# Three weight panels abreast behind each inner norm, and a fourth from tiles of its own, in a hybrid decoder layer

## The reference

```python
def layer_norm(x, g, b):
    xf = x.astype(jnp.float32)
    mu = jnp.mean(xf, axis=-1, keepdims=True)
    xc = xf - mu
    var = jnp.mean(xc * xc, axis=-1, keepdims=True)
    return xc * lax.rsqrt(var + LN_EPS) * g + b
...
    m = jnp.concatenate([y_pool, y_sgu], axis=-1) @ w_out
    h = layer_norm(ALPHA * h + m, ln1_g, ln1_b)
    h = layer_norm(ALPHA * h + mem_attend(h, mem_k, mem_v, w_mq, w_mo), ln2_g, ln2_b)
    h = layer_norm(ALPHA * h + peer_ffn(h, peer_wq, peer_subkeys, peer_u, peer_v), ln3_g, ln3_b)
```

## Time and profile before

| | us |
|---|---|
| median of 3 runs (3997.79 to 4003.11) | 3999.24 |
| the profiled execution | 3993.57 |
| its span, first to last instruction | 3991.8 |
| TensorE busy (matmuls) | 3829.6, 96% |
| VectorE busy | 2589.6, 65% |
| ScalarE busy | 1322.9, 33% |
| GpSimd busy | 784.2, 20% |
| load of an output projection panel, issue to landing | 6.1 |

### The profile page before, as it was taken

One profiled execution on the slowest core, in us unless ns is written; L12 is line 12 of the kernel. 1 busy time (PEld: TensorE's weight loads), 2 busy tenths in 40 slices (PEclk: granted clock), 3 DMA queues, 4 the chain that ended last, 5 costly groups with the idle time before them and its releaser, 6 DMA issues.

```text
span 3991.8 us, 61700 instructions
## 1 busy us (share of the span) xinstructions
PE 3829.6 (96%) x24133; PEld 3710.8 (93%) x24133; DVE 2589.6 (65%) x3361; ACT 1322.9 (33%) x1615; POOL 784.2 (20%) x509
## 2 busy tenths in 40 slices
PE   8998999979979979999999999999999999999997
PEld 6798999979857979999999999999999999999997
DVE  3423343351463356678888577777898998889896
ACT  3342222131342133232455422222233333333334
POOL 0000020020000030027300012222433233433440
PEclk9999999989989999999999999999999999999999
DMA  6542332223543212234455799999999999999994
...
DMA packets 392241, 941.40 MB, mean 236 GB/s; under 512 B 24356, under 2 KB 264672, under 8 KB 339992
## 3 DMA queue, kind: packets, MB, share of 16 engines
...
HBM read 865.84 MB, written 72.77 MB: 235 GB/s over the span
## 4 chain that ended last, share of the span: by engine, by line
PE 88%; DVE 5%; DMA 4%; ACT 2%; DVEq 1%; issue 1%; POOL 0%; SPq 0%; ACTq 0%
PE pp L197 25%; PE pp L1163 23%; PE pp L1210 13%; PE pt L1210 7%; PE pl L1210 7%; PE pt L1137 2%; PE pp L816 2%; DMA u_raw<-in_peer_ut 1%; PE pt L816 1%; PE pl L816 1%; DVE gbuf L1989 1%; PE pp L883 1%; DMA kv<-in_cache_mem_k 1%; DMA raw<-in_w_mk 1%; PE pl L845 1%
## 5 line engine op out<-in xcount | busy, mean ns | idle before, releaser
L1163 PE MATMUL pp<-h_hi,ut_hi 128*128 128x384 f32 x2048 | 703.5, 343 | 1.4 <-DVE ut_lo L1887 1.4
L1163 PE MATMUL pp<-h_lo,ut_hi 128*128 128x384 f32 x2048 | 690.2, 337 | 0.0
L1163 PE MATMUL pp<-h_hi,ut_lo 128*128 128x384 f32 x2048 | 688.5, 336 | 0.0
L212 DVE TENSOR_TENSOR w_lo<-raw,w_hi 128x2048 fp32r<-128x2048 f32 x120 | 274.8, 2291 | 470.1 <-ACT w_hi L207 470.1
L1535 ACT ACTIVATE v_hi<-v_raw 128x1024 fp32r<-128x1024 f32 x256 | 271.8, 1062 | 671.6 <-PE pp L1210 491.3
L1887 DVE TENSOR_TENSOR ut_lo<-u_raw,ut_hi 128x1024 fp32r<-128x1024 f32 x256 | 331.8, 1298 | 248.5 <-ACT ut_hi L1503 168.9
L1163 PEld LDWEIGHTS pp<-h_hi,ut_hi 128*128 128x128 f32 x2048 | 385.4, 188 | 2.1 <-DVE ut_lo L1887 1.7
L2012 DVE TENSOR_TENSOR v_lo<-v_raw,v_hi 128x1024 fp32r<-128x1024 f32 x256 | 314.1, 1227 | 110.5 <-ACT v_hi L1535 109.4
L1163 PEld LDWEIGHTS pp<-h_lo,ut_hi 128*128 128x128 f32 x2048 | 385.4, 188 | 0.0
L1163 PEld LDWEIGHTS pp<-h_hi,ut_lo 128*128 128x128 f32 x2048 | 384.7, 188 | 0.0
L207 ACT ACTIVATE w_hi<-raw 128x2048 fp32r<-128x2048 f32 x120 | 229.3, 1911 | 411.2 <-PE pp L197 285.5
...
## 6 DMA issues: line engine op xcount, KB each, us to landing
...
```

What stands on the lines that cost most here:

```text
L212: nc.vector.tensor_tensor(w_lo[:, s], raw[:, s], w_hi[:, s].bitcast(F32), ALU.subtract).then_inc(lo_ready, 1)
L1163: last = mm(pp[0][:, d, 0:N], w[:, d, k, :], x[:, k, S:S + N], start=(k == 0 and w is ut_hi and x is h_hi), stop=(k == KC - 1 and w is ut_lo))
```

## The change

**GpSimd's subtraction goes.** VectorE subtracts the mean itself in `dve_apply`, directly before each `yt`, with a drain between the two. `pool_less_mean` and its semaphore go.

**Splits.** ScalarE splits the second panel behind the norm ahead of the last square and not behind it. Panels three and four get tiles of their own: `wx_hi[0]`, `wx_lo[0]` and `wx_hi[1]`, `wx_lo[1]`, in the space of `y_hi`/`y_lo` that is free by then. ScalarE and VectorE fill the first between the mean copy and the reciprocal, the second in the middle of the norm's loop (after chunk 9 on ScalarE, after chunk 11 on VectorE).

**TensorE.** `behind_norm` multiplies three panels chunk by chunk, the third into `pl`. `fourth_panel` follows, from the `wx` tiles into the two banks of `pt`. The loop of panels goes on from the fifth. In the expert query stage the scorings of the first five panels are written out: the first stands in the middle of the fourth panel, the third in the middle of the fifth; the third panel's queries have a tile of their own, `q2x`.

**Waits.** The cache loads wait for three query panels in place of the projection's end. GpSimd clears its part of `sc` in two pieces, the second after three scorings.

Its core (the rest changes counts of semaphores and the number of panels skipped):

```diff
+        def pe_panel(pe, u, x_hi, x_lo, first=False, n=T, middle=None):
...
+                if middle is not None and k == KC // 2:
+                    middle()
...
+        def act_split_ahead(act, u):
+
+            s = u % 2
+            act.wait_ge(raw_in[s], num(u)[2])
+            act.wait_ge(panel_done, u - 2 - s)
+            nc.scalar.activation(wx_hi[s][:, :, :], raw[:, s], ACT.Copy).then_inc(hi_ready, 1)
+
+        def dve_split_ahead(dve, u):
+
+            s = u % 2
+            dve.wait_ge(hi_ready, u + 1)
+            nc.vector.tensor_tensor(wx_lo[s][:, :, :], raw[:, s], wx_hi[s][:, :, :].bitcast(F32),
+                                    ALU.subtract).then_inc(lo_ready, 1)
...
+                    if less:
+                        nc.vector.tensor_tensor(buf[:, c, :], buf[:, c, :], flat(mu[:, :, :]), ALU.subtract)
+                        dve.drain()
                     nc.vector.tensor_tensor(yt[:, c % 2, :], buf[:, c, :], flat(rs[:, :, :]), ALU.mult)\
                         .then_inc(nsem["yt"], 1)
...
             pairs(act, u0, KC, body, skip_first=4)
+            act_split(act, num(u0 + KC + 1))
             act_square(act, nm, KC - 1, 1)
-            act_split(act, num(u0 + KC + 1))
             act_mean(act, nm)
+            act_split_ahead(act, u0 + KC + 2)
...
-        def pool_less_mean(pool, nm, buf=r):
-            nm.wait(pool, "mu_out", 1)
-            for c in range(KC):
-                nc.gpsimd.tensor_tensor(buf[:, c, :], buf[:, c, :], flat(mu[:, :, :]), ALU.subtract).then_inc(less_mu, 1)
...
+        wx_hi = [at("wx_hi0", Y_HI + 40960, [P, KC, P], FR), at("wx_hi1", Y_HI + 17408, [P, KC, P], FR)]
+        wx_lo = [at("wx_lo0", Y_HI + 49152, [P, KC, P], FR), at("wx_lo1", Y_HI + 25600, [P, KC, P], FR)]
+        q2x = at("q2x", Y_HI + 33792, [P, T])
...
-                    sp.wait_ge(panel_done, WO0 + 16)
+                    sp.wait_ge(panel_done, MQ0 + 3)
...
-            def first_two(u0, nm):
-
-                pe.wait_ge(lo_ready, u0 + 2)
+            def behind_norm(u0, nm):
+
                 pe.wait_ge(evacuated, u0)
                 for k in range(KC):
                     nm.wait(pe, "used", k + 1)
-                    for s in range(2):
-                        for w, x in ((w_hi, h_hi), (w_hi, h_lo), (w_lo, h_hi)):
-                            for b in range(2):
-                                last = mm(pp[s][:, b, 0:HT], w[:, s, k, :], x[:, k, b * HT:(b + 1) * HT],
-                                          start=(k == 0 and w is w_hi and x is h_hi),
-                                          stop=(k == KC - 1 and w is w_lo))
+                    for s in range(3):
+                        if k == 0:
+                            pe.wait_ge(lo_ready, u0 + s + 1)
+                        hi, lo = ((w_hi[:, s, k, :], w_lo[:, s, k, :]) if s < 2 else (wx_hi[0][:, k, :], wx_lo[0][:, k, :]))
+                        for b in range(2):
+                            mm((pp[0], pp[1], pl)[s][:, b, 0:HT], hi, h_hi[:, k, b * HT:(b + 1) * HT], start=(k == 0), stop=False)
+                        for b in range(2):
+                            mm((pp[0], pp[1], pl)[s][:, b, 0:HT], hi, h_lo[:, k, b * HT:(b + 1) * HT], start=False, stop=False)
+                        for b in range(2):
+                            last = mm((pp[0], pp[1], pl)[s][:, b, 0:HT], lo, h_hi[:, k, b * HT:(b + 1) * HT],
+                                      start=False, stop=(k == KC - 1))
                         if k == KC - 1:
                             last.then_inc(panel_done, 1)
+
+            def fourth_panel(u0, ks):
+
+                pe.wait_ge(lo_ready, u0 + 4)
+                for k in ks:
+                    for w, x in ((wx_hi[1], h_hi), (wx_hi[1], h_lo), (wx_lo[1], h_hi)):
+                        for b in range(2):
+                            last = mm(pt[b][:, 0:HT], w[:, k, :], x[:, k, b * HT:(b + 1) * HT],
+                                      start=(k == 0 and w is wx_hi[1] and x is h_hi), stop=(k == KC - 1 and w is wx_lo[1]))
+                if ks[-1] == KC - 1:
+                    last.then_inc(panel_done, 1)
 
             def summed(u0, n, x_hi, x_lo, buf, nm):
 
@@ -997,8 +1027,9 @@
             out_part(0, range(6, 8), last=True)
             out_part(1, range(4, 8), last=True)
             squared(WO0, norm1, begun=2)
-            first_two(MQ0, norm1)
-            pairs(pe, MQ0, 16, lambda u, c: pe_panel(pe, u, h_hi, h_lo), skip_first=2, issued=2)
+            behind_norm(MQ0, norm1)
+            fourth_panel(MQ0, range(KC))
+            pairs(pe, MQ0, 16, lambda u, c: pe_panel(pe, u, h_hi, h_lo), skip_first=4, issued=4)
...
-            first_two(WQ0, norm2)
+            behind_norm(WQ0, norm2)
...
-            def select_scores(u, s, first=False):
+            def select_scores(u, s, q=None, first=False):
                 pe.wait_ge(evacuated, u + 1)
-                if not first:
+                if first:
+                    pe.wait_ge(evacuated, WQ0 + 3)
+                else:
                     pe.wait_ge(sc_out, u - WQ0)
+                if q is None:
+                    q = q2[:, s, :]
                 for t in range(NT):
-                    mm(pl[:, 0, t * P:(t + 1) * P], q2[:, s, t * P:(t + 1) * P], sub_t[:, s, :], start=True, stop=True)
-                mm(pl[0:NS, 1, 0:P], q2[:, s, SEQ:T], sub_t[:, s, :], start=True, stop=True).then_inc(sc_done, 1)
+                    mm(pl[:, 0, t * P:(t + 1) * P], q[:, t * P:(t + 1) * P], sub_t[:, s, :], start=True, stop=True)
+                mm(pl[0:NS, 1, 0:P], q[:, SEQ:T], sub_t[:, s, :], start=True, stop=True).then_inc(sc_done, 1)
+            fourth_panel(WQ0, range(KC // 2))
             select_scores(WQ0, 0, first=True)
-            with pe.Fori(1, 8) as i:
+            fourth_panel(WQ0, range(KC // 2, KC))
+            select_scores(WQ0 + 1, 1)
+            pe_panel(pe, num(WQ0 + 4), h_hi, h_lo, middle=lambda: select_scores(WQ0 + 2, 0, q=q2x))
+            select_scores(WQ0 + 3, 1)
+            pe_panel(pe, num(WQ0 + 5), h_hi, h_lo)
+            select_scores(WQ0 + 4, 0)
+            with pe.Fori(3, 8) as i:
                 for d in range(2):
                     pe_panel(pe, in_loop(WQ0, i, d), h_hi, h_lo)
...
+            act_apply(act, norm1, ln_g[:, 0, :], ln_b[:, 0, :], h_hi,
+                      after=lambda c: act_split_ahead(act, MQ0 + 3) if c == 9 else None)
...
+            def two_banks(bank):
+                return bank[:, :, 0:HT]
+
+            for c, bank in enumerate((pp[0], pp[1], pl, pt2)):
+                if c == 3:
+                    act_split(act, num(MQ0 + 4))
+                act.wait_ge(panel_done, MQ0 + c + 1)
+                f(qt[:, c, :].rearrange("p (b t) -> p b t", b=2), two_banks(bank), ACT.Copy).then_inc(evacuated, 1)
+            pairs(act, MQ0, 14, panel(q_use), skip_first=4, issued=4)
...
-            panel(wq_use, split=False)(num(WQ0), 0)
-            pairs(act, WQ0, 14, panel(wq_use), skip_first=2, issued=1)
+            for c, (bank, q) in enumerate(((pp[0], q2[:, 0, :]), (pp[1], q2[:, 1, :]), (pl, q2x[:, :]))):
+                act.wait_ge(panel_done, WQ0 + c + 1)
+                f(q.rearrange("p (b t) -> p b t", b=2), two_banks(bank), ACT.Copy).then_inc(evacuated, 1)
+            act_split(act, num(WQ0 + 4))
+            scores_out(0)
+            act.wait_ge(panel_done, WQ0 + 4)
+            act.wait_ge(sc_done, 2)
+            f(q2[:, 1, :].rearrange("p (b t) -> p b t", b=2), two_banks(pt2), ACT.Copy).then_inc(evacuated, 1)
+            scores_out(1)
+            act_split(act, num(WQ0 + 5))
+            scores_out(2)
+            act_split(act, num(WQ0 + 6))
+            act.wait_ge(panel_done, WQ0 + 5)
+            f(q2[:, 0, :].rearrange("p (b t) -> p b t", b=2), two_banks(pp[0]), ACT.Copy).then_inc(evacuated, 1)
+            scores_out(3)
+            act.wait_ge(iota_ready, 2)
+            panel(wq_use, split=False)(num(WQ0 + 5), 5)
+            pairs(act, WQ0, 14, panel(wq_use), skip_first=6, issued=6)
...
-                dve_apply(dve, nm, r, h_lo, h_hi, less=less)
+                dve_split_ahead(dve, u0 + KC + 2)
+                dve_apply(dve, nm, r, h_lo, h_hi, less=True,
+                          after=lambda c: dve_split_ahead(dve, u0 + KC + 3) if c == 11 else None)
             dve.drain()
-            residual_norm(WO0, norm1, 0)
-            pairs(dve, MQ0, 14, lambda u, c: split_next(u), skip_first=2, issued=1)
+            residual_norm(WO0, norm1)
+            pairs(dve, MQ0, 14, lambda u, c: split_next(u), skip_first=4, issued=3)
...
-            for c in range(2 * PH - 1):
-                if 1 <= c < 2 * PH - 1:
-                    split_next(num(WQ0 + c))
-                if c >= 2:
-                    half_list(c - 2)
+            for c in range(3):
+                split_next(num(WQ0 + 3 + c))
+                half_list(c)
+            half_list(3)
+            for c in range(6, 2 * PH - 1):
+                split_next(num(WQ0 + c))
```

(7 more changed lines are left out.)

24 lines of the change are left out of this document (9 added, 15 removed).

## The result

| | before | the change |
|---|---|---|
| median of 4 runs | 3998.51 us (3997.09 to 4003.11) | 3974.12 us (3971.08 to 3980.41) |
| ratio to before, 95% interval | | 0.9938 (0.9926 to 0.995) |
| profiled execution, its span | 3993.57, 3991.8 | 3980.41, 3978.7 |

The change makes the kernel 24.4 us faster by the medians. 3974 was forecast, 3966 to 3984 as the range. That the median falls within 0.2 us of the forecast is luck: the four executions of the change alone lie 9 us apart. Two slow executions, one of `again` (6344 us, granted clock 0.56) and one of before beside it (4780 us, 0.75), are left out of every figure here. I ran the unchanged kernel of the change once more under the label `again`; its profile is the cleaner one, and where it is used, it says so.

What follows compares the result with a forecast made beforehand. TensorE's own work was taken as the bound, with time won only at its waits or half clock. Norm gains of 14.4 and 11.2 us, 25.6 together, move the median from 3999.24 to 3973.6, said as 3974, range 3966 to 3984.

Steps and rivals of the forecast that it cites:

- The bound: Whole kernel: time is won only where TensorE waits or runs at half clock; the norms' gains move rigidly to the end.
- Restart: Behind each norm: TensorE starts 18.4 us after the projection's last panel, 3.1 sooner.
- hide in waits: In the norm: the splits of panels two and three fit into waits of ScalarE and VectorE and cost 0.3 us.
- Three panels abreast: Behind the norm: TensorE's 2.26 us a chunk exceeds VectorE's 2.09, so TensorE is the bound from its first chunk.
- the cover: In the three-panel loop: `h_lo` 10 is ready 1 to 2 us before TensorE wants it, despite the fourth panel's splits.
- Half clock: At TensorE's restart behind each norm: 1.2 GHz for a few us, losing 1.7 to 3.0 us.
- Fourth panel: Behind the three panels: 12.04 us more without a wait, so the old 4.9 us gap is gone.
- A: Three-panel loop: VectorE bounds it; at 2.6 us a chunk 4.5 us late per norm, time 3983; chance 0.12.
- B: Three-panel loop: TensorE's clock stays at half; 4008 with one norm hit, 4042 with both; chance 0.04.
- C: Behind the second norm: VectorE's lists eat that norm's 11.2 us gain; time 3985; chance 0.05.
- D: Third panel's load not in `raw` when its split wants it; were it 12 us late, 3998; chance 0.05.
- the estimate by halves of the ports: Norm, old kernel: were VectorE and GpSimd sharing bandwidth, passes take 1.44 us, gain some 3 us a norm less.

Runs made afterwards that it cites:

- before2: The kernel before the change, unedited, profiled a second time; 3999.02 us.
- after: The kernel of the change in its first profiled execution; 3980.41 us, span 3978.7.
- sub_only: The kernel before the change with only the mean's subtraction moved to VectorE, two panels and no splits ahead; 3993.63 us, ratio 0.9989.
- three_mq: The change without the fourth panel ahead in the first norm, second norm as in the change; 3979.8 us, ratio 0.995.
- later: The change with the third panel's splits and VectorE's fourth-panel split moved later, no added matmuls; 3970.34 us, ratio 0.9931.
- warm: The change with 100 unused matmuls added on TensorE between the last statistics and the first chunk; 3971.51 us, ratio 0.9931.
- warm_end: `warm` with VectorE's split of the fourth panel behind the last chunk, not behind chunk 11; 3969.41 us, ratio 0.9925.
- before3: The kernel before the change, unedited, profiled a third time; 4003.12 us.
- pass_more: The change with one more unused VectorE pass in each chunk of both norms; 3991.32 us, ratio 0.9976.
- pool_back: The change with the mean's subtraction given back to GpSimd, panels and splits kept; 3981.44 us, ratio 0.9953.

## Why the prediction was right

**The bound.** That only TensorE's waits and clock around the norms count, and that all behind them moves rigidly: held as far as the scatter lets one see. The tail was 2295.6 to 2298.9 us in the eight profiles with the new arrangement, 2291.7, 2297.8 and 2298.4 in the three of before; that `before2` and `again` differ by only 0.1 us outside the norms is chance.

**Restart.** 18.4 us after the panel's end forecast, 18.44 to 18.46 in after, `again`, `sub_only` and `three_mq`. The passes are 0.72 to 0.73 and start 0.64 and 0.79 apart; the product of the variance takes 0.73. Held in each step. The restart came where it was forecast, since the splits' length was in the sum. But the reading that they "hide in waits" and cost 0.3 us was wrong: `later` is 1.7 us sooner without them in front of the reciprocal. The new row in front of it was shorter than the old one all the same, and the rest of the gain was left there.

**Three panels abreast.** 56.2 to 57.5 us forecast, 57.3 and 56.3 to 56.6 measured, 57.4 in the second norm of `three_mq`. TensorE was the bound from its first chunk, as said, and no wait stands in after's chain. The reason that I gave for the cover was incomplete: 1 to 2 us at chunk 10 holds only since TensorE loses 1.7 to 2.8 us at its start. With the clock full (`warm`) the mid-loop split costs 0.8. Two losses cover each other, and taking away one alone pays less than its size.

**Half clock.** 1.7 to 3.0 forecast, 2.7 in the first norm and 1.7 to 1.9 in the second measured against `warm_end`, 2.8 in the second norm of `three_mq`. The prediction read 6.0 us of half clock in one norm of before and 3.5 in the other and kept both ends for each; the runs bear that out.

**Fourth panel.** No wait, 12.03. The 2.2 us of dip behind the old gap (1.7 to 1.8 in `before2` and `before3`), given to the change as part of its gain, went with it; `three_mq` (3.64 of wait and 1.8 of dip) and `sub_only` (1.7 of dip) show that the dip belongs to the gap.

**Ends.** Queries done at 213 to 214: 213.85. Expert columns at 234 to 235: 234.1 and 233.8. Norm gains of 14.4 and 11.2 forecast, 14.0 and 11.3 between the first two profiles, 13.4 and 11.6 between `before2` and `again`. The waits that the prediction placed for the panels behind the fourth in the expert query projection didn't come: behind its restart TensorE has no wait in it.

**To the median.** The sum was made against a profiled execution that stood 5.7 under the median, and the same difference was carried over to it. That was right for a reason that I didn't know then: the shortness lay in the tail (6 to 7 us), which the change doesn't touch. For the profiled execution itself the sum said 3968.0, and 3980.41 came, with 6 us more in attention and 5 in the tail; a forecast of one execution could not have been made to that accuracy. The criterion "wrong if the stretch from the first expert column to the end is over 3 us longer", however, was met by the first profile of after (2296.6 against 2291.7) while the forecast held. It was a bad criterion: this stretch scatters from 2289.3 to 2298.9 by itself, and it was set from a single execution.

**The rivals.** A did not happen, and `pass_more` gives its price at a chunk of 2.71 us. The prediction's own formula for it holds there: counted from the panel's end, `h_lo` 13 at the restart of 20.2 plus 13 x 2.71 plus 2.5, and three chunks of 2.26 behind it, give 64.7; measured 64.9 and 64.5. B: the clock was full again within 6 us, and stayed so even where TensorE waits before every chunk, as the window of `pass_more` shows:

```profile
840.00:850.00 10.00, 9.27 (x68) 8.41 (x67) 9.78 (x16) 6.24 (x8) 0.00 (x0) 1.00 0.01 2
```

The slowing at each wait between bursts, which the Trainium skill (TensorE: Matmul & The Clock Gate, HAM oscillation — how this bites in real kernels) describes, is seen here behind the 13 us waits and the 4 us gap, not at the short ones.

C: the second norm kept its gain up to the first expert column (11.3 to 11.6 us), and the tail behind it is as long in `before2` as in `again`, so the lists didn't eat it. D: the third panel's matmuls ran without a wait. In the estimate by halves of the ports, which was not used in the sum, nine passes of 1.87 - 1.44 us are 3.9 us and not some 3.

**How the gain splits.** Profiles, first norm and second: subtraction alone 3.3 and 2.8; panels and splits alone (`pool_back`) 10.2 and 6.7; both 14.0 and 11.3 to 11.6. The parts add up to 13.5 and 9.5, so doing both gives somewhat more than their sum, in the second norm by some 2 us, of which the scatter can be about 1.

What stays open: why the clock granted in the attention stage was 0.86 in one execution of the same program and 0.95 in another, and what makes the tail 2289 to 2299. `later` together with the added matmuls was not run; it would combine a restart at 16.8 with the full clock. Nor was the second panel's earlier split taken back by itself: that it is worth nothing alone but clears VectorE's row is argued from the rows and not shown.
